# Retention: the prompt's value and state products as three passes on split operands

## What is computed

```python
def retention_block(q, k, v, s, log_gamma):
    ...
    scores = jnp.einsum('blhd,bmhd->bhlm', q, k) * decay[None]
    intra = jnp.einsum('bhlm,bmhv->blhv', scores, v)
    ...
    s_new = s * jnp.exp(L * log_gamma)[None, :, None, None] + jnp.einsum(
        'blhd,blhv->bhdv', k * k_decay[None, :, :, None], v)
    return intra + cross, s_new
```

## Time and profile before

| | us |
|---|---|
| median of 3 runs | 1516.46 |
| lowest, highest | 1514.05, 1516.68 |
| the profiled execution | 1516.42 |
| its span, first to last instruction | 1514.5 |
| TensorE busy in it | 1485.4 (98%) |
| VectorE, ScalarE, GpSimd busy | 819.7, 653.9, 294.0 |

### The profile page before, as it was taken

The page is one execution under the profiler, slowest core; times in us unless marked ns, Lnnn a source line. Parts: engine busy times, 40 slices in busy tenths (PEclk is TensorE's granted clock), DMA queues, the critical chain, the costliest instruction groups (busy, mean ns, idle before and its releaser), DMA issues.

```text
span 1514.5 us, 21705 instructions
## 1 busy us (share of the span) xinstructions
PE 1485.4 (98%) x7942; PEld 1136.3 (75%) x7942; DVE 819.7 (54%) x1429; ACT 653.9 (43%) x1073; POOL 294.0 (19%) x177
## 2 busy tenths in 40 slices
PE   8999999999999999999999999999999999999998
PEld 6775777577757775788787677677888988887886
DVE  3432341234124412322675877745465799988998
ACT  5323312321232113312446455545333388888883
POOL 1342134213421342233100000000232100001003
PEclk9999999999999999999999999999999999999999
DMA  9555455555555655433431254154851799999996
GB/s 344 176 155 179 159 184 156 179 166 185 155 172 167 198 149 165 156 105 108 172 128 54 82 164 161 42 160 154 296 138 42 238 365 402 403 362 404 395 392 235
DMA packets 152224, 304.58 MB, mean 201 GB/s; under 512 B 16621, under 2 KB 46189, under 8 KB 151737
## 3 DMA queue, kind: packets, MB, share of 16 engines
q1 hardware_dynamic: 148314, 292.72, 57.0%
q0 software_dynamic: 3808, 10.49, 1.9%
HBM read 258.45 MB, written 47.86 MB: 202 GB/s over the span
## 4 chain that ended last, share of the span: by engine, by line
PE 45%; DMA 3%; DVE 2%; issue 1%; ACT 1%; POOL 0%; DVEq 0%; ACTq 0%; SPq 0%; POOLq 0%
PE pj L93 11%; PE pj L95 11%; PE pj L94 11%; DMA m_raw<-w 2%; PE d_B L2690 1%; PE d_B L2709 1%; PE d_B L2717 1%; PE d_B L2751 1%; DMA d_kc<-cache_diff_k 1%; PE d_B L2699 1%; PE d_B L2857 1%; PE d_B L2678 1%; PE d_B L2728 1%; PE d_B L1721 1%; PE pj L1704 0%
## 5 line engine op out<-in xcount | busy, mean ns | idle before, releaser
L93 PE MATMUL pj<-ring_hi,hT_hi 128*128 128x512 f32 x880 | 368.1, 418 | 2.8 <-ACT d_q_rows L2152 2.3
L95 PE MATMUL pj<-ring_hi,hT_lo 128*128 128x512 f32 x880 | 345.2, 392 | 0.0
L94 PE MATMUL pj<-ring_lo,hT_hi 128*128 128x512 f32 x880 | 344.6, 392 | 0.0
L531 POOL TENSOR_TENSOR ring_lo<-ring_raw,ring_hi 128x1024 fp32r<-128x1024 f32 x79 | 191.4, 2426 | 490.5 <-ACT ring_hi L605 490.3
L605 ACT ACTIVATE ring_hi<-ring_raw 128x1024 fp32r<-128x1024 f32 x79 | 83.4, 1059 | 357.2 <-DMA ring_raw<-w_in 344.6
L1581 DVE TENSOR_TENSOR m_lo<-m_raw,m_hi 128x1024 fp32r<-128x1024 f32 x188 | 222.1, 1220 | 19.3 <-ACT m_hi L1487 18.2
L1487 ACT ACTIVATE m_hi<-m_raw 128x1024 fp32r<-128x1024 f32 x188 | 193.0, 1059 | 22.6 <-DMA m_raw<-w 19.8
L93 PEld LDWEIGHTS pj<-ring_hi,hT_hi 128*128 128x128 f32 x880 | 166.0, 189 | 45.7 <-issue 12.0
L95 PEld LDWEIGHTS pj<-ring_hi,hT_lo 128*128 128x128 f32 x880 | 165.6, 188 | 36.6
L94 PEld LDWEIGHTS pj<-ring_lo,hT_hi 128*128 128x128 f32 x880 | 166.4, 189 | 28.5 <-issue 1.0
L803 DVE SCALAR_TENSOR_TENSOR r_S<-r_S,g,r_sm 128x512 f32<-128x512 f32 x64 | 45.0, 744 | 135.2 <-PE r_sm L1040 135.2
(11 more groups left out here) (387 smaller groups left out, 2430.7 us busy)
## 6 DMA issues: line engine op xcount, KB each, us to landing
m_raw<-w SPq DMA_DIRECT2D x188, 512.0 KB, 10.1
ring_raw<-w_in SPq DMA_DIRECT2D x72, 512.0 KB, 3.8
r_S<-state_ret SPq DMA_DIRECT2D x64, 256.0 KB, 4.6
r_ada_raw<-w_ada SPq DMA_DIRECT2D x16, 1024.0 KB, 6.7
o_state_s<-r_S SPq DMA_DIRECT2D x64, 256.0 KB, 4.2
a_raw<-w_ada SPq DMA_DIRECT2D x8, 1024.0 KB, 12.6
ring_raw<-w_in SPq DMA_DIRECT2D x32, 256.0 KB, 3.6
ring_raw<-w_br_ret SPq DMA_DIRECT2D x16, 512.0 KB, 4.2
```

The costliest lines, as they stand in the source:

```text
L93: pe.matmul(out, s_hi, m_hi, start=start, stop=False)
L94: pe.matmul(out, s_hi, m_lo, start=False, stop=False)
L95: return pe.matmul(out, s_lo, m_hi, start=False, stop=stop)
L531: pool.tensor_tensor(lo[:, p], raw[:, p], hi[:, p].bitcast(F32), ALU.subtract).then_inc(lo_done, 1)
```

## The change

`values` and `state` use `mm3` in place of one float32 matmul, on high and low parts of scores, decayed keys and values:

```diff
+                pe.wait_ge(sc_low, h + 1)
                 for j in range(i + 1):
                     bank_taken(pe, f"V{h}", j)
-                    job_taken(pe, "C", h, j)
-                    c = scoff[j] + (i - j) * P
-                    last = pe.matmul(pj[i][:], scT[:, c:c + P], v[:, j], start=(j == 0), stop=(j == i))
+                    b = scoff[j] // P + i - j
+                    high = qk_r[:, b // 2, 0, b % 2 * P:(b % 2 + 1) * P]
+                    last = mm3(pe, pj[i][:], high, sc_lo[:, b * P:(b + 1) * P], v_hi[:, j], v_lo[:, j], j == 0, j == i)
...
             def state(h, d):
                 out = small("S", h, d)
-                pe.wait_ge(kd_done, h * NP_T + NP_T)
+                pe.wait_ge(kd_low, h + 1)
                 for t in range(NP_T):
-                    last = pe.matmul(out[:], qk[:, t, 1, d * P:(d + 1) * P], v[:, t], start=(t == 0), stop=(t == NP_T - 1))
+                    s = slice(d * P, (d + 1) * P)
+                    last = mm3(pe, out[:], kd_hi[:, t, s], qk_r[:, t, 1, s], v_hi[:, t], v_lo[:, t], t == 0, t == NP_T - 1)
```

The parts are made on ACT and DVE. Values: ACT writes the high part straight from the bank, DVE subtracts it and frees the bank. Scores and keys: ACT writes both high parts after its fourth `split_hi` of Gh, DVE the low parts between the second and the third `update`:

```diff
+            def high_parts(h):
+                job_taken(act, "C", h, 2)
+                job_taken(act, "C", h, 3)
+                act.activation(qk_r[:, :, 0], scT[:, 0:1280].rearrange("p (t c) -> p t c", c=RDK), ACT.Copy).then_inc(sc_hi, 1)
+                act.wait_ge(kd_done, (h + 1) * NP_T)
+                act.wait_ge(z_done, 5 * h + 2)
+                act.activation(kd_hi[:], qk[:, 0:NP_T, 1], ACT.Copy).then_inc(kd_high, 1)
...
-                    ins = act.activation(v[:, t], pj[t][:], ACT.Copy)
-                    if t == NP_T:
+                    if t < NP_T:
+                        act.activation(v_hi[:, t], pj[t][:], ACT.Copy).then_inc(v_split, 1)
+                    else:
+                        act.activation(v[:, t], pj[t][:], ACT.Copy)
                         if h:
                             act.wait_ge(vk_out, 128 * h)
-                        ins = act.activation(v4_hi[:], pj[t][:], ACT.Copy)
-                    ins.then_inc(pj_free[t], 1)
+                        act.activation(v4_hi[:], pj[t][:], ACT.Copy).then_inc(pj_free[t], 1)
...
+            def low_v(h, t):
+                dve.wait_ge(v_split, h * NP_T + t + 1)
+                dve.tensor_tensor(v_lo[:, t], pj[t][:], v_hi[:, t].bitcast(F32), ALU.subtract).then_inc(pj_free[t], 1)
...
+            def low_parts(h):
+                dve.wait_ge(sc_hi, h + 1)
+                dve.tensor_tensor(sc_lo[:].rearrange("p (t c) -> p t c", c=RDK), scT[:, 0:1280].rearrange("p (t c) -> p t c", c=RDK),
+                                  qk_r[:, :, 0].bitcast(F32), ALU.subtract).then_inc(sc_low, 1)
+                dve.wait_ge(kd_high, h + 1)
+                dve.tensor_tensor(qk_r[:, 0:NP_T, 1], qk[:, 0:NP_T, 1], kd_hi[:].bitcast(F32), ALU.subtract).then_inc(kd_low, 1)
```

More of the change, by code:

```diff
@@ L220, in phase_r @@
         qkT = sb("r_qkT", [P, 4, NT * P], F32)
+        qk_r = nc.alloc_sbuf_tensor_at("r_qk_split", [P, NT, 2, RDK], F32R, offset=K.after_acc_ret)
+        S_p = sb("r_S_p", [P, 2, RDV], F32, at=sb.at - 4 * NT * P * 4)
+        kd_hi = sb("r_kd_hi", [P, NP_T, RDK], F32R, at=sb.at - 4 * NT * P * 4 + 4096)
+        v_hi = sb("r_v_high", [P, NT, RDV], F32R, at=sb.at)
         v = sb("r_v", [P, NT, RDV], F32)
@@ L224, in phase_r @@
         scT = sb("r_scT", [P, 1280 + P], F32)
+        sc_lo = sb("r_scT_lo", [P, 1280], F32R, at=at_scT)
         tmp = sb("r_tmp", [P, 2, W], F32, at=at_scT)
@@ L235, in phase_r @@
         k4_lo = sb("r_k4_lo", [P, RDK], F32R)
-        S_p = sb("r_S_p", [P, 2, RDV], F32)
+        v_lo = sb("r_v_low", [P, NP_T, RDV], F32R)
         uraw = sb("r_ada_raw", [P, KT, UW], F32)
-        sb.at = K.phase_base + 106496
         rope = sb("r_rope", [P, NT, 2, P], F32)
@@ L281, in phase_r @@
         roped, kd_done, z_done, qz_set = map(sem, ("qk_roped", "kd_done", "z_done", "qz_set"))
+        v_split, sc_hi, sc_low, kd_high, kd_low = map(sem, ("v_hi_done", "scT_hi_done", "scT_lo_done", "kd_hi_done", "kd_lo_done"))
         v4_split, vk_out, vk_in = map(sem, ("v4_split", "vk_out", "vk_in"))
@@ L626, in squares @@
                 act.activation(S_sq[:], bank[:], ACT.Square, accum_out=st[:, 0, t:t + 1]).then_inc(sumsq, 1)
+            def high_parts(h):
[5 more added lines that the diff above has]
+                act.activation(kd_hi[:], qk[:, 0:NP_T, 1], ACT.Copy).then_inc(kd_high, 1)
             def take_state(h, d):
                 job_done(act, "S", h, d)
-                if h:
-                    act.wait_ge(Sp_out, 32 * h)
                 act.activation(S_p[:, d], job_bank("S", h, d)[:], ACT.Copy).then_inc(job_free("S", h, d), 1)
@@ L698, in _ @@
                     bank_done(act, f"V{h}", t)
-                    ins = act.activation(v[:, t], pj[t][:], ACT.Copy)
-                    if t == NP_T:
+                    if t < NP_T:
+                        act.activation(v_hi[:, t], pj[t][:], ACT.Copy).then_inc(v_split, 1)
+                    else:
+                        act.activation(v[:, t], pj[t][:], ACT.Copy)
                         if h:
                             act.wait_ge(vk_out, 128 * h)
-                        ins = act.activation(v4_hi[:], pj[t][:], ACT.Copy)
-                    ins.then_inc(pj_free[t], 1)
+                        act.activation(v4_hi[:], pj[t][:], ACT.Copy).then_inc(pj_free[t], 1)
                 split_hi(f"G{h}", 3)
+                high_parts(h)
                 follow = f"QK{h + 1}" if h + 1 < RH else "GR0"
@@ L787, in rotate @@
                 dve.tensor_tensor(ae[:, :, 1], t1[:, :, 1], t2[:, :, 0], ALU.add).then_inc(roped, 1)
+            def low_v(h, t):
[7 more added lines that the diff above has]
+                dve.tensor_tensor(qk_r[:, 0:NP_T, 1], qk[:, 0:NP_T, 1], kd_hi[:].bitcast(F32), ALU.subtract).then_inc(kd_low, 1)
             def take_T(h, t):
                 job_done(dve, "T", h, t)
+                if h and t == ROPE_ORDER[0]:
+                    dve.wait_ge(Sp_out, 32 * h)
                 dve.tensor_copy(qkT[:, :, t * P:(t + 1) * P], job_bank("T", h, t)[:].rearrange("p (k c) -> p k c", c=P)) \
@@ L879, in _ @@
                         take_T(h, t)
+                for t in range(NP_T):
+                    low_v(h, t)
                 for j in (4, 0, 1, 2, 3):
@@ L882, in _ @@
                 for i in range(8):
+                    if i == 2:
+                        low_parts(h)
                     update(h, i)
```

## The result

The changed kernel takes 1504.53 us (median of 4 runs, 1504.09 to 1506.24) where the kernel before, run beside it, takes 1516.03 (4 runs, 1514.05 to 1516.68). The ratio is 0.9928, 95% interval 0.9915 to 0.994: 11.5 us faster by the medians, where 12.5 were forecast. The forecast of 1503.9 is 0.6 us off.

A forecast was written before the change was run, and what follows sets the result against it. TensorE's instruction list was taken as the bound, busy 1485.4 of 1514.5 us. Savings of 1.74, 0.70 and 0.69 make 3.13 us per head, 12.5 in four: 1516.46 - 12.5 = 1503.9 us, range 1501.5 to 1508.5.

The forecast's parts named there:

- TensorE's list sets the end: Phase R and behind it: TensorE's own instruction list sets the time, so a microsecond taken out should come off.
- `values` 8.58 to 6.84: `values`, per head: 30 fp32r matmuls at 0.228 us replace ten float32 matmuls, 1.74 us less.
- First `state` to 2.83: `state(h, 0)`, per head: 3.53 us becomes 2.83, 0.70 less, including 0.09 for the step to a narrow matmul.
- Second to 2.94: `state(h, 1)`, per head: 3.63 us becomes 2.94, 0.69 less, including 0.20 for standing between narrow jobs.
- Sum 3.13 a head, stretch 13.60: First `values` matmul to end of `state(h, 1)`: 16.73 us becomes 13.60, saving 3.13 per head, 12.5 in four.
- Twelve passes into one bank: `values` and `state`: up to 12 fp32r matmuls accumulating into one bank cost between 0.228 and 0.392 us each; 0.228 taken.
- Rival 3: Accumulating 12 times into one bank is slow, 0.392 us a matmul: 5.4 us a head more, 1538 in all; chance 0.03.
- The parts are hidden: Splitting values, scores and keys into high and low parts on ACT and DVE costs nothing; each has time to spare.
- DVE against POOL: During G0: low scores, POOL, low keys, updates block each other until 126.9; TensorE asks at 127.53, so no cost.
- What is late next: the state tiles: `cross(h, 2)` comes 2.44 us sooner; head 2 closest, 1.2 us to spare; a 6 us landing would cost 0.8 there.
- no wait of TensorE in the trace: Support for the sum holding, 1501.5 to 1506.5 us, chance 0.80: TensorE's longest wait totals 4.2 us, once.
- the second rival: DVE and POOL contention stalls TensorE up to 1.5 us a head, or state loads come late: 1506.5 to 1510; chance 0.12.

The follow-up runs named there:

- four passes: Changed kernel with a fourth pass, low x low, added in `values`: 1513.41 us, ratio 0.9975 to the kernel before.
- moving it away: Changed kernel with the low parts made ahead of the first update instead of the third, before POOL's pieces come: 1505.85 us, ratio 0.9924.
- four more subtractions: Changed kernel with four unused 480-column subtractions added on DVE between low scores and low keys: 1530.39 us, ratio 1.0089.
- steps sooner: Changed kernel with the first pair of sample steps (`r_vk` jobs) moved up to contraction step 3, before its data can be there: 1524.6 us, one run.
- one pass: Changed kernel with only the high x high pass in `values` and `state`, low parts made but left out: 1502.48 us, ratio 0.9916.
- states early: Changed kernel with the state tiles for `cross(h, 2)` loaded one ring piece (two contraction steps) earlier: 1504.48 us, ratio 0.9927.
- both moves: Changed kernel with sample steps one contraction step later and state tiles loaded two contraction steps earlier: 1500.22 us, ratio 0.9897.

## Why the prediction was right, point by point

- **TensorE's list sets the end**: right. 40 added passes came out as 9.75 us by the medians (7 by the ratios) for 9.1, and D moved as a block (10.5 at the barrier, 10.2 at the end).
- **`values` 8.58 to 6.84**: measured 6.80 in both profiles of the kernel. **First `state` to 2.83**: 2.81 in head 1 (291.15 to 293.96). **Second to 2.94**: 2.95. **Sum 3.13 a head, stretch 13.60**: 3.18 and 13.55.
- **Twelve passes into one bank**, the unseen price: 0.227, the lower end. Rival 3 is dead; with four passes 16 in a row cost the same.
- **The parts are hidden**: right at all three places. The values' low parts end at 96.1 with TensorE standing nowhere, the high parts at 115.2 (116.5 forecast), the low parts and updates at 125.7 (126.9 forecast).
- **DVE against POOL** (low scores, POOL, low keys, POOL): came in that order in head 0, with low keys 3.42 us in the mean of four heads. That it is free was only argued in the forecast; moving it away (1505.85) bears it out, and adding work to it (1530.39) shows that it is free only while the updates end before TensorE asks. The Trainium skill, SBUF — State Buffer, "Who interferes with whom", has who interferes: an instruction of VectorE with two SBUF inputs and one of GpSimd that reads SBUF, the one that starts first blocking the other for its whole length. The trace agrees: 3.41 is 1.22 and a wait of 2.2 for one piece of POOL.
- **What is late next: the state tiles**: the right suspect, with the wrong margin. The forecast took head 2 as the closest, with 1.2 us to spare, and a landing half as long again at 6 us as the bad case. In the changed kernel the slowest landings of the heads were 7.3, 5.8, 6.0 and 5.8 us, and it was head 0 that stood, 0.64 us. The landing of one load in one head was used as if it were a constant, where the same trace of before had 5.7, 6.1, 4.8 and 5.5 us as the slowest of the four loads of heads 0 to 3. One pass in place of three shows the same limit at 20.3 us.
- **What the forecast didn't have at all: the clock.** It priced a late wait by its length. In these runs waits above 1.6 us were often, and those above 3 us always, followed by half clock, so that they cost up to twice their length (the last section has the count). The trace of before had shorter waits for `r_vk`, three of 2.2 us in all, which the forecast passed over with "no wait of TensorE in the trace". The clock is the largest of the losses of head 0. With four waits of 3.1 us in place of the second rival's 1.5 it doubled their cost; at 1.5 us itself no half clock was seen, so the rival's 1506.5 to 1510 may have held.

The measured gain of 11.5 lies 1 us below the 12.5. The waits for `r_vk` and `r_S` with their half clock, which cost the one profiled execution 3.1 us (0.64 + 0.9 + 1.6) more than the other, are large enough to make that difference; whether they do in the runs without a profile can't be seen.

## What to carry to other kernels

A float32 matmul with 512 columns is 0.858 us of a stream here, an fp32r pass 0.227: three passes on split operands win a fifth of it, four lose, and the splitting must be free, on engines and in buffers that have time. Before believing the sum, look for the next late thing at the place where time is taken out, by the longest landing in several traces and not by one. And price a wait of TensorE in the middle of dense work, when it grows beyond some 1.6 us as here, by more than its length. When you can, put work that needs a late transfer one step further down the list, which here gave some 2 us for nothing, at the edge of what these runs can tell.

## What was not expected of the hardware

**The granted clock falls behind a wait in the middle of a dense program.** Over all 13 traces, from 15 us on, TensorE stood for more than 1 us 88 times. Behind the 45 waits of 1.03 to 1.56 us the clock never fell. Behind the 31 of 1.62 to 2.43 us it fell to the half level 14 times and stayed at full level 17 times. With the 12 of 3.09 to 5.39 us (four more subtractions, steps sooner, one pass) it fell every time, during the wait or behind it, and was at half for 3 to 7 us. What decides in the middle group isn't settled here: the first `r_vk` job waited 1.71, 1.69 and 1.76 us with half clock behind it (changed kernel, four passes, states early), and 1.75 us with full clock behind it (four more subtractions, 1.00 in 118.2 to 121.8).

**It explains differences between executions of one kernel.** Apart from the last microseconds of the program, every stretch at half clock in the 13 traces stands at one of these waits. So does the granted clock of 0.76 in 20.0 to 24.6 us, in the execution of before and in that of the kernel with both moves (1.00 in the other eleven): it follows waits of 2.25 and 2.13 us for `a_raw`, while waits of 2.17 and 2.03 us at the same place (changed kernel, steps sooner) had full clock behind them. One such stretch is worth 1 to 2 us, as much as some of the effects looked for here.
